# Last layer norm: sample tile first, two rows of a token added by one product, the norm spread over VectorE, ScalarE and GpSimd

## The reference

```python
def layer_norm(x, g, b):
    mu = jnp.mean(xf, -1, keepdims=True)
    var = jnp.mean(jnp.square(xf - mu), -1, keepdims=True)
    return ((xf - mu) * lax.rsqrt(var + LN_EPS) * g + b)
...
    x = layer_norm(DEEPNORM_ALPHA * x + gt2 * hier_moe(h2, ...), ln2_g, ln2_b)
```

## Time and profile before

| | before |
|---|---|
| median of 3 runs | 720.27 us (716.08 to 723.23) |
| the profiled execution's own time | 721.39 us |
| its span, first to last instruction | 719.6 us |
| busy: TensorE matmul, VectorE, ScalarE, GpSimd | 595.0, 335.8, 135.2, 103.2 us |
| mean granted TensorE clock | 0.92 |
| moved by DMA | 180.98 MB, 252 GB/s on average |
| last expert scatter issued | 677.76 us |
| five loads of expert rows issued | from 680.46 us |
| last VectorE instruction starts | 715.94 us |

### The profile page before, as it was taken

The page is one execution under the profiler, slowest core; times in us unless marked ns, Lnnn a source line. Parts: engine busy times, 40 slices in busy tenths (PEclk is TensorE's granted clock), DMA queues, the critical chain, the costliest instruction groups (busy, mean ns, idle before and its releaser), DMA issues.

```text
span 719.6 us, 10926 instructions
## 1 busy us (share of the span) xinstructions
PE 595.0 (83%) x4530; PEld 373.0 (52%) x4530; DVE 335.8 (47%) x600; ACT 135.2 (19%) x356; POOL 103.2 (14%) x144
## 2 busy tenths in 40 slices
PE   3679999899987687999836999887788887769884
PEld 2559999676764364444525655443344444335330
DVE  2463441555542662595685344433333333343348
ACT  1441450244332153011111100000000000000100
POOL 3000000100001013000021233222222222212100
PEclk9969999999998599999955999999998999999996
DMA  8991321002006989810399799999999999996162
GB/s 299 370 247 60 68 63 56 16 1 102 16 1 237 364 319 261 301 56 32 134 409 369 290 414 412 411 410 408 411 412 410 410 409 409 407 405 271 48 248 96
DMA packets 71289, 180.98 MB, mean 252 GB/s; under 512 B 22165, under 2 KB 26109, under 8 KB 66629
## 3 DMA queue, kind: packets, MB, share of 16 engines
q1 hardware_dynamic: 60612, 163.39, 60.9%
q0 software_dynamic: 7936, 14.09, 5.6%
q10 hardware_dynamic: 2688, 2.77, 1.1%
HBM read 176.25 MB, written 14.45 MB: 265 GB/s over the span
## 4 chain that ended last, share of the span: by engine, by line
PE 46%; SPq 27%; DMA 10%; DVE 10%; ACT 4%; issue 3%; DVEq 0%; POOLq 0%; ACTq 0%
SPq L431 27%; PE bank L947 8%; PE bank L1193 8%; PE bank L1014 6%; PE bank L1297 5%; DMA ring<-in_moe_w_up_dram 3%; DMA ring<-in_ada_w_dram 3%; PE bank L1371 3%; PE bank L901 2%; PE bank L1315 2%; PE bank L996 2%; DMA x_tok<-in_x_sample_dram 2%; PE bank L1038 1%; PE bank L1055 1%; PE bank L1283 1%
## 5 line engine op out<-in xcount | busy, mean ns | idle before, releaser
L1297 PE MATMUL bank<-late_w,xT 128*64 128x256 f32 x672 | 83.4, 401 | 20.9 <-DMA late_w<-in_moe_w_up_dram 18.0
L1799 DVE COPY xT<-bank 128x512 f32<-128x512 f32 x38 | 26.2, 692 | 125.0 <-PE bank L1283 124.4
L1297 PE MATMUL bank<-ring,xT 128*64 128x256 f32 x480 | 64.7, 426 | 20.4 <-DMA ring<-in_moe_w_up_dram 18.6
L1297 PEld LDWEIGHTS bank<-late_w,xT 128*64 128x64 f32 x672 | 49.6, 139 | 60.9 <-DMA late_w<-in_moe_w_up_dram 28.6
L1297 PEld LDWEIGHTS bank<-ring,xT 128*64 128x64 f32 x480 | 36.9, 148 | 52.2 <-DMA ring<-in_moe_w_up_dram 27.6
L843 ACT ACTIVATE sgl<-bank 128x128 f32<-128x128 f32 x36 | 10.0, 277 | 246.9 <-PE bank L1297 246.8
L602 POOL DMA_INDIRECT expert_rows<-ye,dsti x36 | 36.5, 1014 | 125.7 <-DVE ye L1818 125.7
L595 POOL DMA_INDIRECT xg<-h_scratch,srci x38 | 39.2, 1031 | 102.5 <-PE bank L1283 89.0
L1815 DVE SCALAR_TENSOR_TENSOR S<-bank,modrt,S 128x512 f32<-128x512 f32 x36 | 27.0, 750 | 32.6 <-PE bank L1315 32.3
L1315 PE MATMUL bank<-late_w,hT 128*64 128x512 f32 x168 | 40.7, 605 | 0.0
L1014 PE MATMUL bank<-ring_r,h_high 128*128 128x512 f32 (+1 forms) x140 | 38.2, 413 | 0.0
(11 more groups left out here) (315 smaller groups left out, 860.2 us busy)
## 6 DMA issues: line engine op xcount, KB each, us to landing
ring<-in_ada_w_dram SPq DMA_DIRECT2D x22, 1024.0 KB, 11.1
late_w<-in_moe_w_gate_dram SPq DMA_DIRECT2D x21, 1024.0 KB, 16.8
late_w<-in_moe_w_up_dram SPq DMA_DIRECT2D x21, 1024.0 KB, 22.4
late_w<-in_moe_w_down_dram SPq DMA_DIRECT2D x21, 1024.0 KB, 22.4
ring<-in_moe_w_down_dram SPq DMA_DIRECT2D x15, 1024.0 KB, 22.7
ring<-in_moe_w_gate_dram SPq DMA_DIRECT2D x15, 1024.0 KB, 16.5
ring<-in_moe_w_up_dram SPq DMA_DIRECT2D x15, 1024.0 KB, 22.6
ring<-in_w_in_dram SPq DMA_DIRECT2D x7, 1024.0 KB, 5.6
```

The source lines that it names most:

```text
L1297: mm = pe.matmul(bank[2 + a][f * C:(f + 1) * C, 0:2 * P], x, w[:, kk, f, :, :], start=(kk == 0), stop=(kk == KD - 1))
```

## The change

**Order of tiles.** `FINAL` is [4, 0, 1, 2, 3]: loads, sums, statistics and stores take the sample tile first. Positions in this order are called q.

**Layout of the rows.** `expert_rows` now has 2176 rows of 2 KB. For 64 prompt tokens the 64 first-choice rows are followed by the 64 second-choice rows, and the sample's 32 and 32 lie at the end. A load brings, for each group of 64 tokens u = 0, 1 of a prompt tile, 128 partitions of 4 KB: the first choices on partitions 0 to 63, the second ones on 64 to 127. For the sample tile it is 64 partitions of 4 KB. VectorE computes `dsti` for this layout with five instructions of 48 columns in place of one.

**The sum.** `twice` is a 128 x 64 matrix with two ones in each column, made by GpSimd with its other constants, so that one product adds the two rows of 64 tokens. A prompt tile takes four products for x and four for the rows, each with 64 output partitions; before, it was two and four with 128. The sample tile takes two and two.

**The norm.** VectorE computes the statistics and a negated mean; ScalarE computes the root, the negated mean times it, and then (two instructions of 512 columns, out of PSUM into `x_tok`) the normalised sum; VectorE multiplies with the gain (`times_g`); GpSimd adds the bias, but for the last tile, where VectorE does. The fifth tile's banks are free as soon as ScalarE has read the first tile's.

```diff
--- before.py
+++ after.py
-    yb_d = nc.dram_tensor("expert_rows", [4 * KSTEP, HALF], f32).ap()
+    YROWS = 2 * (2 * LP + 2 * LS)
+    yb_d = nc.dram_tensor("expert_rows", [YROWS, HALF], f32).ap()
+    FINAL = [T // P] + list(range(T // P))
...
+        twice = sb("twice", [P, CH])
+        twice_s = sb("twice_s", [2 * LS, LS])
...
-            rows2 = yb_d.rearrange("(k t h) n -> t k (h n)", k=2, h=2)
-            for j in range(NT):
-                sp.dma_start(ring[0:ROWS[j], j, :].rearrange("p (k n) -> p k n", k=2),
-                             rows2[P * j:P * j + ROWS[j], :, :]).then_inc(s_fin[j], 16)
-            for j in range(NT):
-                sp.wait_ge(f_o, j + 1)
+            rows2 = yb_d.rearrange("(r h) n -> r (h n)", h=2)
+            for j in FINAL:
+                if j < NP:
+                    sp.dma_start(ring[:, j, :].rearrange("p (u n) -> p u n", u=2),
+                                 rows2[2 * P * j:2 * P * (j + 1), :].rearrange("(u p) n -> p u n", u=2)).then_inc(s_fin[j], 16)
+                else:
+                    sp.dma_start(ring[0:2 * LS, j, 0:D], rows2[2 * LP:2 * LP + 2 * LS, :]).then_inc(s_fin[j], 16)
+            for q, j in enumerate(FINAL):
+                sp.wait_ge(*((f_o, q + 1) if q < NT - 1 else (f_last, 1)))
...
+            link(pool.tensor_tensor(twice[:, :], ident[:, 0:CH], ident[:, CH:P], ALU.add))
+            link(pool.tensor_tensor(twice_s[:, :], ident[0:2 * LS, 0:LS], ident[0:2 * LS, LS:2 * LS], ALU.add))
...
+            pool.wait_ge(s_ln2, 32)
+            for q, j in enumerate(FINAL[:-1]):
+                x = x_tok[0:ROWS[j], j, :]
+                pool.wait_ge(f_g, q + 1)
+                pool.tensor_tensor(x, x, ln2[0:ROWS[j], 1, :], ALU.add).then_inc(f_o, 1)
...
-            for j in range(NT):
-                v = stat[0:ROWS[j], j % 2, 13:14]
-                act.wait_ge(f_v, j + 1)
-                act.activation(v, v, ACT.Sqrt).then_inc(f_l, 1)
+            for q, j in enumerate(FINAL):
+                r = ROWS[j]
+                st = stat[0:r, q % 2, :]
+                act.wait_ge(f_v, q + 1)
+                act.activation(st[:, 13:14], st[:, 13:14], ACT.Sqrt).then_inc(f_l, 1)
+                act.wait_ge(f_l, q + 1)
+                act.activation(st[:, 14:15], st[:, 14:15], ACT.Identity, scale=st[:, 13:14]).then_inc(r_chain, 1)
+                act.wait_ge(r_chain, q + 1)
+                for half in range(2):
+                    act.activation(x_tok[0:r, j, half * 512:(half + 1) * 512], bank[SUM_BANKS[q][half]][0:r, :], ACT.Identity,
+                                   scale=st[:, 13:14], bias=st[:, 14:15]).then_inc(f_z, 1)
...
-            def sum_out(j):
-                return [bank[i][0:ROWS[j], :] for i in SUM_BANKS[j]]
-            def sum_x(j):
-                r = ROWS[j]
-                for half, out in enumerate(sum_out(j)):
-                    pe.matmul(out, ident[0:r, 0:r], x_tok[0:r, j, half * 512:(half + 1) * 512], start=True, stop=False)
+            def sum_x(q):
+                j = FINAL[q]
+                for half in range(2):
+                    out, c = bank[SUM_BANKS[q][half]], slice(half * 512, (half + 1) * 512)
+                    if j < NP:
+                        for u in range(2):
+                            pe.matmul(out[u * CH:(u + 1) * CH, :], ident[:, u * CH:(u + 1) * CH], x_tok[:, j, c], start=True, stop=False)
+                    else:
+                        pe.matmul(out[0:LS, :], ident[0:LS, 0:LS], x_tok[0:LS, j, c], start=True, stop=False)
+            def sum_rows(q):
+                j = FINAL[q]
+                pe.wait_ge(s_fin[j], 16)
+                for half in range(2):
+                    out = bank[SUM_BANKS[q][half]]
+                    if j < NP:
+                        for u in range(2):
+                            c = u * D + half * 512
+                            mm = pe.matmul(out[u * CH:(u + 1) * CH, :], twice[:, :], ring[:, j, c:c + 512], start=False, stop=True)
+                    else:
+                        mm = pe.matmul(out[0:LS, :], twice_s[:, :], ring[0:2 * LS, j, half * 512:(half + 1) * 512], start=False, stop=True)
+                mm.then_inc(pe_sum, 1)
 
             pe.wait_ge(x_al, NT)
-            for j in range(3):
-                sum_x(j)
-            for j in range(NT):
-                r = ROWS[j]
-                pe.wait_ge(s_fin[j], 16)
-                if j >= 3:
-                    if j == 4:
-                        pe.wait_ge(f_o, 1)
-                    sum_x(j)
-                for k in range(2):
-                    for half, out in enumerate(sum_out(j)):
-                        c = k * D + half * 512
-                        mm = pe.matmul(out, ident[0:r, 0:r], ring[0:r, j, c:c + 512], start=False, stop=(k == 1))
-                mm.then_inc(pe_sum, 1)
+            pe.wait_ge(pl, NPAIRS)
+            for q in range(3):
+                sum_x(q)
+            for q in range(NT):
+                if q == 3:
+                    pe.wait_ge(s_fin[FINAL[q]], 16)
+                    sum_x(q)
+                if q == 4:
+                    pe.wait_ge(f_z, 2)
+                    sum_x(q)
+                sum_rows(q)
...
-            link(dve.tensor_copy(dsti[:, :], ent[:, :]))
+            dve.wait_ge(tbl_ready, 1)
+            link(dve.tensor_scalar(dsti[:, :], srci[:, :], -2 * CH, None, ALU.bitwise_and))
+            link(dve.tensor_scalar(behind, srci[:, :], float(2 * LP), -2.0 * LS, ALU.is_ge, ALU.mult))
+            link(dve.scalar_tensor_tensor(behind, behind, 2.0 * CH, second_row, ALU.add, ALU.mult))
+            link(dve.scalar_tensor_tensor(behind, behind, -1.0 / (2 * KSTEP), srci[:, :], ALU.mult, ALU.add))
+            link(dve.tensor_tensor(dsti[:, :], behind, dsti[:, :], ALU.add))
...
-            def spread(j):
-                st = stat[0:ROWS[j], j % 2, :]
-                dve.wait_ge(pe_sum, j + 1)
-                link(dve.bn_stats(st[:, 0:6], bank[SUM_BANKS[j][0]][0:ROWS[j], :]))
-                link(dve.bn_stats(st[:, 6:12], bank[SUM_BANKS[j][1]][0:ROWS[j], :]))
+            def spread(q):
+                r = ROWS[FINAL[q]]
+                st = stat[0:r, q % 2, :]
+                dve.wait_ge(pe_sum, q + 1)
+                link(dve.bn_stats(st[:, 0:6], bank[SUM_BANKS[q][0]][0:r, :]))
+                link(dve.bn_stats(st[:, 6:12], bank[SUM_BANKS[q][1]][0:r, :]))
                 link(dve.bn_aggr(st[:, 12:14], st[:, 0:12]))
+                link(dve.tensor_scalar(st[:, 14:15], st[:, 12:13], -1.0, None, ALU.mult))
                 link(dve.tensor_scalar(st[:, 13:14], st[:, 13:14], EPS, None, ALU.add))
                 dve.reciprocal(st[:, 13:14], st[:, 13:14]).then_inc(f_v, 1)
 
-            def normalised(j):
+            def times_g(q):
+                j = FINAL[q]
                 x = x_tok[0:ROWS[j], j, :]
-                st = stat[0:ROWS[j], j % 2, :]
-                for half in range(2):
-                    c = slice(half * 512, (half + 1) * 512)
-                    link(dve.scalar_tensor_tensor(x[:, c], bank[SUM_BANKS[j][half]][0:ROWS[j], :], st[:, 12:13], ln2[0:ROWS[j], 0, c],
-                                                  ALU.subtract, ALU.mult))
-                dve.wait_ge(f_l, j + 1)
-                dve.scalar_tensor_tensor(x, x, st[:, 13:14], ln2[0:ROWS[j], 1, :], ALU.mult, ALU.add).then_inc(f_o, 1)
-            for j in range(NT + 1):
-                if j < NT:
-                    if j >= 2:
-                        dve.wait_ge(f_o, j - 1)
-                    spread(j)
-                if j >= 1:
-                    normalised(j - 1)
+                dve.wait_ge(f_z, 2 * (q + 1))
+                dve.tensor_tensor(x, x, ln2[0:ROWS[j], 0, :], ALU.mult).then_inc(f_g, 1)
+                if q == NT - 1:
+                    dve.wait_ge(f_g, NT)
+                    dve.tensor_tensor(x, x, ln2[0:ROWS[j], 1, :], ALU.add).then_inc(f_last, 1)
+            for q in range(NT + 1):
+                if q < NT:
+                    spread(q)
+                if q >= 1:
+                    times_g(q - 1)
```

More of the change, by code:

```diff
@@ L160, in hymba_stream_step @@
         second_row = rt[:, 9, 0:NBLK]
+        behind = rt[:, 9, NBLK:2 * NBLK]
         weight_hot = rt[:, 0:3, :].rearrange("p i n -> p (i n)").rearrange("p (i n) -> p i n", i=2 * NT)
@@ L268, in hymba_stream_step @@
         f_v, f_l, f_o = sem("final_var"), sem("final_rstd"), sem("final_out")
+        f_z, f_g, r_chain, f_last = sem("final_scaled"), sem("final_times_g"), sem("final_rstd_chain"), sem("last_tile_out")
         y_part = sem("ye_parts")
@@ L480, in _ @@
             sp.wait_ge(s_out, 16 * NT)
-        NCONST, NSLOT = 24, 30
+        NCONST, NSLOT, NPAIRS = 24, 30, 32
         @block.gpsimd
@@ L604, in scatter @@
                     in_=ye[:, a, :], in_offset=None,
-                    bounds_check=4 * KSTEP - 1, oob_is_err=False).then_inc(s_sc[a], 16)
+                    bounds_check=YROWS - 1, oob_is_err=False).then_inc(s_sc[a], 16)
             gather(0, 0)
```

## The result

The changed kernel takes 714.73 us (median of 20 runs, 711.71 to 719.9) against 720.5 us (20 runs, 715.6 to 724.4) for the kernel before: ratio 0.9935, 95% interval 0.991 to 0.996. That is 0.65% faster, within the 1% that the prediction called "no change". The ratio is that of the two means (715.04 and 719.75 us); the medians alone are 5.8 us or 0.8% apart, and further down too a ratio can differ from the quotient of two medians, by up to 0.3%. The forecast was 711.0 us, 1.3% faster. The time lies in the range, the ratio shows half of the predicted gain, and one more mechanism is at work than the prediction had.

A forecast was written before the change was run, and what follows sets the result against it. The prediction took the 39 us last layer norm, with TensorE and VectorE about level, as the bound. Span end moving from 719.6 to 710.3 gains 9.3 us; median 720.27 less 9.3 gives 711.0 us, range 707 to 716.

The forecast's parts named there:

- What bounds the kernel: Last layer norm: a 39 us stretch with nothing else left, TensorE (5.15 us) and VectorE (4.85 us) about level per tile.
- its price is zero up to 3.45 us an addition: GpSimd's bias additions in the tail: taken as 2.3 us each, once in 3.44 us, so costing nothing.
- The end: After VectorE's last instruction at 707.2: 2.4 us plus 0.7 for the larger store, span end 710.3, gain 9.3 us.
- The mutual blocking: Tail: VectorE and GpSimd exclude each other when both read two SBUF tiles; 2.0 us lost, 713.0 us; chance 0.25.
- The full clock in t0's rows: First prompt tile's row sums: shorter TensorE pause keeps the clock at 1.00, VectorE starts 1.7 us earlier, 709.2; chance 0.15.
- The loads: Start of the tail: sample tile's 256 KB, now first, lands at 683.85; prompt tiles from 686.35 to 693.9.
- GpSimd's addition and ScalarE's products: Tail norm: a bias addition taken as 2.3 us between 0.96 and 4.6; ScalarE's two products 0.80 us each.
- the slow addition: GpSimd's bias additions in the tail take up to 4.6 us each, giving 715.6 us; chance 0.06.
- the rival on the other side: Tail sums on TensorE: paired products do not overlap, each costs a 0.86 us slot, giving 721.9 us; chance 0.03.
- TensorE at 1.2 GHz to the end: Tail sums: TensorE stays at the low clock since it does less, giving 717.9 us; chance 0.05.
- The routing: Ahead of the experts: five small VectorE instructions add 0.9 us, hidden behind the wait for gathered rows; price nothing.
- faster by more: Whole kernel: chance 0.69 of a gain above about 1% (7.2 us), from forecast, full clock, routing and half of blocking.

The follow-up runs named there:

- late memset: Kernel before, plus GpSimd waiting for VectorE's last result and then setting one column of a constant; 728.13 us against 720.21, ratio 1.0108.
- run with memsets: Changed kernel with GpSimd's four bias additions replaced by memsets of an idle tile, result not valid; only profiled, span end 36.8 us after the last scatter.
- second run with two additions: Changed kernel with GpSimd adding the bias for two tiles only and VectorE for three, measured again in more executions; 711.0 us against 719.99, ratio 0.9902.
- split alone: Kernel before, with its old layout, order, loads and products, given only the new norm over three engines; 723.64 us, ratio 1.0057.
- sums alone: Changed kernel's layout, order and products with the old norm, nothing on GpSimd, against the kernel before; 715.79 us against 720.81, ratio 0.9944.

## Why the prediction was wrong

**What bounds the kernel** was read rightly: the tail is a stretch of its own, the two engines were level in it, and the part between the last scatter and VectorE's last instruction fell from 39.5 to 30.1 us. The prediction's own sequence had 707.2 - 677.76 = 29.4, 0.7 us less.

**The step that failed** is the one on GpSimd: "its price is zero up to 3.45 us an addition", and with it "The end", which was made of VectorE's last instruction and the store alone. The prediction looked at GpSimd only as a supplier of the stores. GpSimd now works until 27.8 us after the last scatter, and its closing takes 8.9 us more. The late memset showed that this closing alone can hold the whole kernel; with two additions left the DRAIN ends before the store has landed, and the end comes 0.4 us after the landing, as in the prediction's sum. Taken from the changed kernel: 36.9 - 32.8 - 0.4 = 3.7 us of the 9.3 forecast were lost in it; VectorE's 0.7 us are the rest, and 4.9 are left. The prediction named slow additions, late ones and blocked ones among its rivals, but none in which a duly fast GpSimd ends the program.

**The mutual blocking** was a rival at 0.25, and it came true, on top of the step that failed. Forecast were 0.23 us on each of three tiles and 1.35 at the end, 2.0 together; measured against 1.21 to 1.23 for a free product are 0.3, 0.2 and 0.2, and 1.55 for the last one, 2.3 us. The third of the small ones is not on the path, since VectorE then waits 0.73 us for ScalarE, so 2.1 us count. The run with memsets gives 1.9. Had GpSimd's closing not been there, this rival's 713.0 would have been 1.4 us too high: VectorE's gain of 9.4 us, less 0.7 for the longer store, is 8.7, and 720.3 - 8.7 = 711.6. Half of that is the earlier start of the first prompt tile, below. Most of the rest is that a tile without blocking takes 3.28 us (691.90 to 695.18) where 3.44 was forecast. Neither this rival nor the forecast had the closing.

**The full clock in t0's rows** was the rival at 0.15, and its outcome came true in all the kernels with the new sums, though in this execution not by the way it named. The granted clock (busy times of five engines, then clock, DMA share, GB/s):

```profile
682.00:684.00 2.00, 2.00 (x6) 0.47 (x4) 0.00 (x0) 0.00 (x0) 0.00 (x0) 0.50 0.21 80
...
686.00:688.00 2.00, 2.00 (x9) 0.50 (x6) 0.00 (x0) 0.00 (x0) 0.00 (x0) 0.78 1.03 383
...
690.00:692.00 2.00, 1.56 (x8) 0.29 (x4) 1.83 (x7) 0.00 (x0) 0.00 (x0) 1.00 1.05 420
```

It was low while the x products ran, 0.50 at 682:684, and they took 8.8 us here, from 679.07 to 687.8, where the prediction kept the 7.02 us of the run before; it was 1.00 in 690:692 and stayed so to the end of the sums. That the x products would be done at 683.6 again was therefore wrong here, and there was no pause of 0.8 us as the rival had it: they ended 1.0 us after the sample's rows had landed. In the second run with two additions they took 7.2 us (674.49 to 681.64), TensorE paused 0.3 us, and the clock was 1.00 from 680:682 on, which is the rival's way. With the split alone, which has the old sums, TensorE was idle for 3.9 us ahead of the rows (to 682.40), and the clock stood at 0.50 in 684:686 again. So the sample tile's rows started late (687.79, although landed by 686.8), and those of t0 fast. The first statistics of t0 followed those of the sample without a gap. Together VectorE's first prompt tile began 11.4 us after the last scatter, where 12.1 was predicted.

**The loads**: the sample tile's 256 KB landed 3.6 us after their issue; forecast was 683.85 - 680.46 = 3.4.

```profile
ring<-expert_rows SPq DMA_DIRECT2D x4, 1024.0 KB, 8.8
...
ring<-expert_rows SPq DMA_DIRECT2D x1, 256.0 KB, 3.6
```

**GpSimd's addition and ScalarE's products**: 2.35 us, where 2.3 was taken between 0.96 and 4.6. An estimate of 2.25 us came from the Trainium skill, GPSIMD Engine Reference, section 3.1; the trace has 0.1 us more. ScalarE's products took 0.77 us each, 0.80 forecast.

```profile
L646 POOL TENSOR_TENSOR x_tok<-x_tok,biasH 128x1024 f32<-128x1024 f32 x3 | 7.0, 2347 | 3.5 <-DVE x_tok L1912 3.5
...
L895 ACT ACTIVATE x_tok<-bank,stat 128x512 f32<-128x512 f32 x8 | 5.8, 773 | 0.1
```

So the slow addition is out, at the upper end of whose range the kernel would have taken 715.6, near what was measured: the same number by a cause that this row excludes.

**The pairs overlap**: eight records in 1.94 us; the rival on the other side is out. So is TensorE at 1.2 GHz to the end.

**The routing** costs next to nothing, as forecast. The five instructions are done at 383.9, the table is ready at 388.9, and the first expert product starts at 389.38, 6.8 us after `srci` begins, where it was 6.7:

```profile
382.54 0.21 DVE L1813 TENSOR_TENSOR srci<-ent,modrt 128x48 int32<-128x48 f32 x1
...
383.71 0.21 DVE L1821 TENSOR_TENSOR dsti<-modrt,dsti 128x48 int32<-128x48 f32 x1
...
388.74 0.17 DVE L1837 CAST ovi<-ent 1x17 int32<-1x17 f32 x1
...
389.38 1.10 PE L1309 MATMUL bank<-ident,xg 128*128 128x128 f32 x4 [3.62 <-DMA xg<-h_scratch,srci]
```

**A slip in the chances.** The prediction's list for "faster by more" adds up to 0.705, not 0.69; nothing hangs on it.

**The parts.** In the profiles, sums alone give 5.9 us, the split alone costs 5.2, both together give 4.9. The split is worth 9.4 - 6.7 = 2.7 us of VectorE's time on top of the sums, and the DRAIN takes all of it and 1.0 us more. With two additions on GpSimd the split gives 2.9 us over the sums alone.

## What to carry to other kernels

Work that GpSimd gets near the end of a program brings its closing there: before moving work to it in the tail, look up how long its DRAIN takes behind its last instruction (here 8.9 us), and let its last instruction end that much before the last store has landed. And where VectorE and GpSimd both run instructions with two SBUF inputs in a tail, read the duration of each instruction, not only the waits: the blocking stood nowhere as a wait, it made a product of 1.22 us one of 2.77.

## What the runs showed of the hardware

GpSimd's closing DRAIN ended 8.9 us after its last instruction in twelve profiles and for three kinds of last instruction: an indirect DMA (8.90), an addition (8.91 to 8.92) and a memset (9.08). VectorE's DRAIN ended 0.05 us after its last instruction in all twelve. One idle column of memset behind the last result cost 7.9 us. What GpSimd does in those 8.9 us was not tried and stays open. Nor could the runs tell why the experts' part ends up to 9 us earlier or later from one profile to the next. The three profiles of the changed kernel and the one with memsets (last scatter at 680.0 to 684.1) are later than all others (674.6 to 679.4). The medians, less tail and 1.8 us, show no such order: an estimate of 673.4 to 677.7 for the changed kernel and 674.8 to 678.5 for the others.
